# A two-block transformer forward pass on one core: a new order of loads, transposes and warming products in its opening

## The reference, cut to what matters

```python
u = rms_norm(h, attn_norm[0])          # h = x, 256 x 1024
y = u @ w_in                           # ab_layer: w_in is 1024 x 2920
aq, ackv, akr, aqi, aki, awi, bq, bk, bv, bf = split_cols(y, AB_WIDTHS)
...
return rms_norm(h, final_norm)         # end of the first block
```

## Time and profile before

| | us |
|---|---|
| time, median of 3 runs | 907.61 (907.19 to 907.74) |
| span of the profiled execution, first to last instruction | 906.0 |
| PE busy | 888.7 (98% of the span) |
| DVE busy | 645.3 (71%) |
| ACT busy | 509.7 (56%) |
| POOL busy | 124.6 (14%) |

### The profile page before, as it was taken

One profiled execution on the slowest core, in us unless ns is written; L12 is line 12 of the kernel. 1 busy time (PEld: TensorE's weight loads), 2 busy tenths in 40 slices (PEclk: granted clock), 3 DMA queues, 4 the chain that ended last, 5 costly groups with the idle time before them and its releaser, 6 DMA issues. The chain is left out here.

```text
span 906.0 us, 14857 instructions
## 1 busy us (share of the span) xinstructions
PE 888.7 (98%) x4796; PEld 743.3 (82%) x4796; DVE 645.3 (71%) x1305; ACT 509.7 (56%) x1017; POOL 124.6 (14%) x168
## 2 busy tenths in 40 slices
PE   8999999999999999999999999999999999999998
PEld 7878787888888888888878888888887778878876
DVE  4768756766666679787467666666876878777785
ACT  6653836445444456686354444444656666666573
POOL 1310300000000000355010000000530401400401
PEclk9999999999999999999999999999999999999999
DMA  9643143656555557101437665555464445454431
GB/s 336 226 150 114 31 157 116 209 191 197 193 188 197 193 186 232 48 25 48 140 116 223 195 189 192 198 185 191 142 221 144 140 140 184 149 179 141 163 116 47
DMA packets 41609, 145.75 MB, mean 161 GB/s; under 512 B 4688, under 2 KB 6224, under 8 KB 41552
## 3 DMA queue, kind: packets, MB, share of 16 engines
q1 hardware_dynamic: 41264, 144.93, 48.2%
q10 hardware_dynamic: 288, 0.07, 0.0%
HBM read 143.93 MB, written 1.05 MB: 160 GB/s over the span
## 5 line engine op out<-in xcount | busy, mean ns | idle before, releaser
L463 DVE TENSOR_TENSOR wl<-raw,wh 128x1024 fp32r<-128x1024 f32 (+2 forms) x270 | 329.3, 1223 | 89.7 <-ACT wh L458 87.0
L458 ACT ACTIVATE wh<-raw 128x1024 fp32r<-128x1024 f32 (+2 forms) x270 | 281.7, 1046 | 66.0 <-PE acc L355 43.3
L353 PE MATMUL acc<-wh,xhl 128*128 128x512 f32 (+1 forms) x472 | 190.8, 404 | 1.3 <-DVE wl L463 0.9
L355 PE MATMUL acc<-wh,xhl 128*128 128x512 f32 (+1 forms) x472 | 184.6, 391 | 0.0
L354 PE MATMUL acc<-wl,xhl 128*128 128x512 f32 (+1 forms) x472 | 184.0, 390 | 0.0
L353 PEld LDWEIGHTS acc<-wh,xhl 128*128 128x128 f32 x472 | 88.7, 188 | 25.8 <-issue 8.0
L355 PEld LDWEIGHTS acc<-wh,xhl 128*128 128x128 f32 x472 | 88.6, 188 | 19.1
L354 PEld LDWEIGHTS acc<-wl,xhl 128*128 128x128 f32 x472 | 88.9, 188 | 16.3
L353 PE MATMUL acc<-wh,hh 128*128 128x512 f32 x256 | 100.2, 392 | 0.0
L354 PE MATMUL acc<-wl,hh 128*128 128x512 f32 x256 | 100.0, 391 | 0.0
L355 PE MATMUL acc<-wh,hl 128*128 128x512 f32 x256 | 99.7, 390 | 0.0
(11 more groups left out here) (302 smaller groups left out, 1350.5 us busy)
## 6 DMA issues: line engine op xcount, KB each, us to landing
raw<-stream SPq DMA_DIRECT2D x266, 512.0 KB, 3.4
raw<-stream SPq DMA_DIRECT2D x4, 352.0 KB, 6.5
h<-x SPq DMA_DIRECT2D x4, 256.0 KB, 4.0
out<-h SPq DMA_DIRECT2D x3, 256.0 KB, 2.1
row<-rows SPq DMA_DIRECT2D x1, 700.0 KB, 9.4
probs<-sel SPq DMA_DIRECT2D x1, 512.0 KB, 8.3
cst<-consts SPq DMA_DIRECT2D x1, 507.0 KB, 7.6
out<-h SPq DMA_DIRECT2D x2, 128.0 KB, 2.0
```

The lines of the kernel that those rows point to most:

```text
L353: nc.tensor.matmul(out_, ah, bh, start=start, stop=False, skip_group_check=True)
L355: return nc.tensor.matmul(out_, al, bh, start=False, stop=stop_, skip_group_check=True)
L458: nc.scalar.activation(used(u, wh[:, u % SPLIT, :]), used(u, raw[:, u % RAW, :]), ACT.Copy).then_inc(w_hi, 1)
L463: nc.vector.tensor_tensor(used(u, wl[:, u % SPLIT, :]), used(u, raw[:, u % RAW, :]), used(u, wh[:, u % SPLIT, :]).bitcast(F32), ALU.subtra ...
```

## The change

SP loads x as four DMAs of 256 columns, both token tiles in each, with one weight unit behind each; the constants come ahead of `col`; of `row` only what lies ahead of the final norm's gain is loaded there; units 5 to 9 are issued by straight code, with the selectors behind unit 7 and the final norm's gain behind unit 9; the loop then starts at unit 10. PE runs 4 pairs of warming products, float32 instead of fp32r, 128 x 64 by 256 columns, one for output partitions 0 to 63 and one for 64 to 127. It transposes one quarter of x (four transposes) ahead of unit 0, and each further quarter behind part 0 of the unit before it. POOL copies the selectors later, and waits for the gain where it is first used.

```diff
-        x_in = sem("x_in0"), sem("x_in1")
+        x_in = [sem(f"x_in{q}") for q in range(4)]
+        fin_in = sem("fin_in")
...
-        WAKE = 10
+        WAKE = 4
...
-            for half in range(2):
-                for t in range(T):
-                    hs = slice(half * 512, (half + 1) * 512)
-                    nc.sync.dma_start(h[:, t, hs], x[t][:, hs]).then_inc(x_in[half], 16)
-                load(half, half)
-            for r in range(2, RAW):
-                load(r, r)
+            for q in range(4):
+                qs = slice(q * 256, (q + 1) * 256)
+                nc.sync.dma_start(h[:, :, qs], x[:, :, qs].rearrange("t p d -> p t d")).then_inc(x_in[q], 16)
+                load(q, q)
+            load(RAW - 1, RAW - 1)
+            nc.sync.dma_start(cst[:, P:], consts_d[:, P:]).then_inc(c_in, 16)
+            nc.sync.dma_start(row[:, 0:R_FIN], rows_d[:, 0:R_FIN]).then_inc(c_in, 16)
             nc.sync.dma_start(col[:, G_MLP0:], cols_d[:, G_MLP0:]).then_inc(col_in, 16)
-            nc.sync.dma_start(cst[:, P:], consts_d[:, P:]).then_inc(c_in, 16)
-            nc.sync.dma_start(sel_stage, sel_d).then_inc(sel_in, 16)
-            nc.sync.dma_start(row[:, :], rows_d).then_inc(c_in, 16)
-            with sp.Fori(0, UNITS // RAW - 1) as lap:
+            for u in range(RAW, 2 * RAW):
+                sp.wait_ge(w_lo, u - RAW + 1)
+                load(u - RAW, u)
+                if u == RAW + 2:
+                    nc.sync.dma_start(sel_stage, sel_d).then_inc(sel_in, 16)
+            nc.sync.dma_start(row[:, R_FIN:], rows_d[:, R_FIN:]).then_inc(fin_in, 16)
+            with sp.Fori(0, UNITS // RAW - 2) as lap:
                 for r in range(RAW):
-                    sp.wait_ge(w_lo, lap * RAW + (r + 1))
-                    load(r, lap * RAW + (r + RAW))
+                    sp.wait_ge(w_lo, lap * RAW + (r + RAW + 1))
+                    load(r, lap * RAW + (r + 2 * RAW))
...
                 for _ in range(n):
-                    mm(bank[:, :], zero[:, 0:P], zero[:, :], start=True, stop=True, skip_group_check=True)
+                    for half in range(2):
+                        mm(bank[64 * half:64 * half + 64, 0:SEQ], zero[:, 0:64].bitcast(F32), zero[:, 0:SEQ].bitcast(F32),
+                           start=True, stop=True, skip_group_check=True)
...
-            def turn_x(half):
+            def turn_x(cc):
 
-                pe.wait_ge(x_in[half], 32)
-                for cc in (2 * half, 2 * half + 1):
-                    for c in range(2):
+                pe.wait_ge(x_in[cc], 16)
+                for c in range(2):
...
             turn_x(0)
-            first_unit(0, (0,))
-            turn_x(1)
-            first_unit(0, (1, 2))
-            for u in range(1, 4):
-                first_unit(u, (0, 1, 2))
+            for u in range(4):
+                first_unit(u, (0,))
+                if u < 3:
+                    turn_x(u + 1)
+                first_unit(u, (1, 2))
...
-            act.wait_ge(x_in[1], 32)
+            for q in range(4):
+                act.wait_ge(x_in[q], 16)
...
-            pool.wait_ge(sel_in, 16)
-            g.tensor_copy(selr[:, :, :].rearrange("p h q -> p (h q)"), sel_stage).then_inc(sel_set, 1)
             pool.wait_ge(c_in, 32)
...
             pool_rsqrt(rr(S_KI), ss(S_KI), HD, pc_.link).then_inc(a_rstd, 1)
+            pool.wait_ge(sel_in, 16)
+            g.tensor_copy(selr[:, :, :].rearrange("p h q -> p (h q)"), sel_stage).then_inc(sel_set, 1)
...
             pool.wait_ge(turned, 20)
+            pool.wait_ge(fin_in, 16)
             g.tensor_tensor(fin2, row[:, R_FIN:R_FIN + D], row[:, R_FIN:R_FIN + D], ALU.mult).then_inc(fin_squared, 1)
```

More of the change, by code:

```diff
@@ L893, in _ @@
             pe.wait_ge(id_in, 32)
-            def turn_x(half):
-                pe.wait_ge(x_in[half], 32)
-                for cc in (2 * half, 2 * half + 1):
-                    for c in range(2):
[L900 to L904, removed]
+            def turn_x(cc):
+                pe.wait_ge(x_in[cc], 16)
+                for c in range(2):
+                    for t in range(T):
+                        f = (2 * cc + c) * P
+                        last = nc.tensor.transpose(opening[cc][:, c * SEQ + t * P:c * SEQ + (t + 1) * P],
+                                                   h[:, t, f:f + P], ident)
+                last.then_inc(turned, 1)
             def first_unit(u, parts):
```

## The result

The changed kernel takes 911.91 us (median of 5 runs, 909.93 to 913.71), the one before 907.41 (907.08 to 907.74). The ratio is 1.0042, 95% interval 1.0029 to 1.0054: 0.42% slower. Forecast was 909.8, range 906.7 to 912.6. The profiled execution is the quickest of the five: 909.93, span 908.1, so 2.1 us over the span before, where 2.2 were forecast. The other 2 us of the median are in runs that have no profile of their own; the experiments say where part of them comes from.

The account below looks back on a forecast made before the run. PE, busy in 98% of the span, was taken as the bound; -0.8 (start) + 2.6 (ring) + 1.7 (sums of squares, split 4) - 1.3 (vanished waits) = +2.2 us, 907.6 to 909.8, 8-in-10 range 906.7 to 912.6.

Parts of the forecast that it names:

- Ring: Units 1 to 3: part 0, transposes and ACT's copies and split wait in turn, 3.10 us a turn, +2.6 us.
- Sums of squares and split 4 in the open: Before unit 4: ACT's sums of squares and split 4 no longer lie under PE's work, +1.7 us.
- Given back: Unit 5 onward: waits vanish, 0.7 us before unit 5, 0.3 before the transposes, 0.3 before the forget sums, -1.3 us.
- Start of unit 0: Opening: with less x ahead of its load, unit 0 starts at 7.75, 0.8 us sooner.
- Warming pairs: Opening: four float32 pairs run side by side on column halves, 3.5 us, ending at 4.8 in place of 5.74.
- Rival (d): Warming: column halves run one behind the other, unit 0 1.65 to 2.9 us later, 911.5 to 912.7; chance 12%.
- my own case: Whole kernel: the main forecast of 909.8 us, own range 909.0 to 910.9, chance 52%.
- rival (c): Opening: after shorter warming PE's clock is not at the upper level by unit 0, 911.5 to 913; chance 10%.
- Rival (a): Opening: loads, not ACT, set the pace, no ring forms, 1.9 us gained, 905.7; chance 12%.
- Rival (b): Opening and the later L974 wait: lateness partly taken up, about half the loss goes, 908.7; chance 14%.

Follow-up runs that it names:

- e10: The kernel before with only PE's interleaving of transposes and units, its loads and ten warming products kept: 911.86 us, ratio 1.0051.
- e2: The changed kernel with the transposes one quarter further ahead on PE, short warming kept: 907.02 us.
- e8: The changed kernel with ACT's two passes of sums of squares behind split 4 in place of ahead of it: 908.8 us.
- e14: The changed kernel with eight more products of zeros on PE between unit 3 and unit 4: 910.21 us.
- e1: The changed kernel with the ten fp32r warming products of before in place of the four float32 pairs: 911.69 us.
- e11: The kernel before with only the later loads (constants and short rows first, selectors behind unit 7, gain behind unit 9, later selector copy): 906.09 us, ratio 0.9984.
- e4: The kernel before with only its warming changed, four float32 pairs on column halves in place of ten fp32r products: 907.45 us.

## Why the prediction was right, and what it missed

- **Ring**, forecast 3.10 us a turn, measured 3.02 (the semaphore to ACT took 0.03, not 0.14). Right; e10 has it without the new loads, e2 takes it away. This is the cause of the loss, and it is shown.
- **Sums of squares and split 4 in the open**: split 4 at 18.65 (18.9 forecast), unit 4 at 21.01 (21.25), PE idle 2.02 us. Right; e8 removes it.
- **Given back**: unit 5 directly behind unit 4, the latent's transposes at 26.59 (27.0 forecast), 2.15 us later than before (24.44), the forget sums 1.9 later, and the span 2.1 longer. Right.
- **Start of unit 0**: 7.78, forecast 7.75. The number was luck: two errors in it cancel. I had the load land at 6.8 and set the pace, with ACT's copies done by 6.4. In the changed kernel unit 0's load was issued at 1.23 and took

```profile
raw<-stream SPq DMA_DIRECT2D x1, 352.0 KB, 3.9
```

so it was there at 5.1, and nobody waited for it. What held unit 0 was PE's first four transposes: 1.10 us in place of the 0.60 I took, with starts 0.21 us apart. Before, eight of them took 1.07 us, 0.11 us apart: the four ran at the lower level. Their result came at 6.01, ACT's copies ran from 6.12 and its split from 6.85. In e14's profile the same four were quicker, and unit 0 started at 7.25:

```profile
4.83 0.66 PE L907 MATMUL pair<-cst,h 128*128 128x128 f32 x4
```

- **Warming pairs**: sixteen instructions in 3.68 us, ending at 4.98: side by side, as taken from the row halves and as the Trainium skill states it (TensorEngine Tiling (Array Packing), Key Properties). Rival (d) is out.
- **The missed term**: 2 us of the median. The medians are 4.5 us apart where 2.2 were forecast, and 911.91 lies outside the range of my own case (909.0 to 910.9). It is inside the stated range only because rivals (c) and (d) had widened that to 912.6: the ring was forecast, this part of the number is luck. I had the clock as rival (c) with one chance in ten, tied it to the shorter warming and to unit 0, and priced it at 1.7 to 3.4 us (its 3.9 us for twelve products would be 3.6 by its own 0.43 against 0.23). One fall cost 1.6 us in e1, about 0.9 in e14. The place was right for e14 and e10, where the fall comes at unit 0, but e1 has it at unit 4, and the changed kernel's profile has none. The shorter warming is not what makes the spread: e1 has it with the long one. I forecast the 2.02 us of idle PE ahead of unit 4 and priced them at their length alone. That the clock falls behind them in some runs is shown in e1; that this made the longer runs of the changed kernel is inferred from e1 and e8 and from the runs' mean clocks, and no profile shows those runs. It is not the whole: about 2 us of the 913.71 are not the clock, and the kernel before, whose long stretch is only the 1.72 us ahead of unit 0, also reads 0.998 or less in 19 of its 77 runs beside the experiments, with three of them at 911.6 to 912.0.
- **Rival (a)**, the loads set the pace: false for the changed kernel, but half true for the kernel before: with the later loads alone e11's median is 1.5 us lower, and 1.1 us of waiting for unit 5 and behind it are gone from its profile. **Rival (b)**: nothing was taken up after 31 us.

## What to carry to other kernels

When a producer's instruction is moved behind a consumer's in one queue, follow the ring through both queues and add up its latencies; if the sum exceeds the work of the bounding engine in one turn, run the producer one step further ahead. An idle stretch of TensorE near 2 us can cost more than its length (1.6 us more in e1); look at the spread of the runs and their mean clocks, and not only at one profile. Before loads are cut finer, move out of their way what nobody needs yet: of this change that was the part worth having.

## What the runs showed of the hardware

- TensorE's granted clock fell to its lower level behind idle stretches of 2.03 us (e1, low from 22.5 to 25.9), 1.76 us (e14, 8.1 to 11.5) and 2.30 us (e10, 8.4 to 11.8), in some executions and not in others; in the changed kernel's profile stretches of 1.76 and 2.02 us passed without it. The fall came when products ran again: 1.3 us behind the first of them in e1, 0.8 in e14, 0.1 in e10. The Trainium skill (TensorE: Matmul & The Clock Gate, Why this matters for your kernels) warns only of gaps between bursts that are longer than any of these; these runs show the fall behind shorter ones, and they decide.
- Unit 0's 352 KB took 3.9 us behind 256 KB of x (changed kernel), 4.9 us in e14 with the same loads ahead, and 5.1 (e4) and 5.9 us (kernel before) behind 512 KB.
- Float32 products on two column halves run side by side: four pairs, sixteen instructions, in 3.68 us at the lower level, where one behind the other they would have needed about 7.
- x's second quarter, 256 KB in pieces of 1 KB with a weight unit ahead of it, took 5.4 us from issue to landing in the changed kernel, its first quarter, with nothing ahead of it, 3.4 us.
